# A token list of its own for the first expert tile in a mixture-of-experts encoder layer

## What is computed

```python
def hier_moe(h, w_group, w_router, w_exp_gate, w_exp_up, w_exp_down):
    gl = t @ w_group                       # 4 groups, top 1
    el = einsum('nd,gde->nge', t, w_router)  # 4 experts in a group, top 2
    ...
    for e in range(16):
        he = jax.nn.silu(t @ w_exp_gate[e]) * (t @ w_exp_up[e])
        out = out + dense_w[:, e:e + 1] * (he @ w_exp_down[e])
```

## Time and profile before

| | us |
|---|---|
| median of 3 runs (lowest to highest) | 902.66 (901.66 to 906.27) |
| the profiled execution | 903.54 |
| its span | 901.70 |
| TensorE busy (share of the span) | 867.5 (96%) |
| VectorE busy | 455.5 (51%) |
| ScalarE busy | 389.2 (43%) |
| GpSimd busy | 181.4 (20%) |
| moved by DMA | 142.47 MB, mean 158 GB/s |

### The profile page before, as it was taken

One profiled execution on the slowest core, in us unless ns is written; L12 is line 12 of the kernel. 1 busy time (PEld: TensorE's weight loads), 2 busy tenths in 40 slices (PEclk: granted clock), 3 DMA queues, 4 the chain that ended last, 5 costly groups with the idle time before them and its releaser, 6 DMA issues.

```text
span 901.7 us, 13646 instructions
## 1 busy us (share of the span) xinstructions
PE 867.5 (96%) x5206; PEld 731.5 (81%) x5206; DVE 455.5 (51%) x747; ACT 389.2 (43%) x539; POOL 181.4 (20%) x129
## 2 busy tenths in 40 slices
PE   8999999999999999999999999999988999899975
PEld 7988888898888888888888888888977878688842
DVE  5411356455519632324232147532588878787617
ACT  6432444444432543434334203124435677677613
POOL 0001010000100001100100001300013786778542
PEclk9999999999999999999999999999989999999998
DMA  9423132232220314321321112792859999988578
GB/s 295 124 69 77 48 76 65 60 69 56 59 71 18 94 47 77 85 63 47 64 61 34 60 47 95 242 395 94 303 195 329 361 381 381 385 306 293 199 258 338
DMA packets 97371, 142.47 MB, mean 158 GB/s; under 512 B 4582, under 2 KB 75446, under 8 KB 97238
## 3 DMA queue, kind: packets, MB, share of 16 engines
q1 hardware_dynamic: 89384, 115.05, 37.8%
q0 software_dynamic: 7904, 26.44, 10.5%
q10 hardware_dynamic: 32, 0.26, 0.3%
HBM read 116.31 MB, written 25.43 MB: 157 GB/s over the span
## 4 chain that ended last, share of the span: by engine, by line
PE 78%; DVE 6%; issue 4%; DMA 4%; SPq 3%; ACT 3%; POOL 2%; ACTq 0%; POOLq 0%; DVEq 0%
PE main L830 20%; PE main L831 19%; PE main L832 19%; PE work L914 3%; PE work L884 2%; PE work L947 2%; PE work L931 2%; PE work L901 1%; PE work L1061 1%; SPq L581 1%; PE work L1114 1%; DMA xg<-h_rows,column 1%; POOL e_lo0d L742 1%; DMA e_raw<-in_w_exp_down 1%; DMA x_in<-in_x_prompt 1%
## 5 line engine op out<-in xcount | busy, mean ns | idle before, releaser
L830 PE MATMUL main<-ht_hi,w_hi 128*128 128x512 f32 (+1 forms) x576 | 198.5, 345 | 0.0
L831 PE MATMUL main<-ht_lo,w_hi 128*128 128x512 f32 (+1 forms) x576 | 194.0, 337 | 0.0
L832 PE MATMUL main<-ht_hi,w_lo 128*128 128x512 f32 (+1 forms) x576 | 193.9, 337 | 0.0
L1512 DVE TENSOR_TENSOR w_lo<-raw,w_hi 128x2048 fp32r<-128x2048 f32 x29 | 66.4, 2290 | 234.9 <-ACT w_hi L1207 234.9
L830 PEld LDWEIGHTS main<-ht_hi,w_hi 128*128 128x128 f32 x576 | 109.2, 190 | 18.7 <-issue 5.2
L832 PEld LDWEIGHTS main<-ht_hi,w_lo 128*128 128x128 f32 x576 | 109.2, 190 | 11.9
L831 PEld LDWEIGHTS main<-ht_lo,w_hi 128*128 128x128 f32 x576 | 109.4, 190 | 10.9
L830 PE MATMUL main<-w_hi,ht_hi 128*128 128x256 f32 (+1 forms) x304 | 95.6, 315 | 0.1
L683 POOL DMA_DIRECT2D bias<-bias_vectors x16 | 12.4, 774 | 408.1 <-DVE nmx L1578 176.4
L832 PE MATMUL main<-w_hi,ht_lo 128*128 128x256 f32 (+1 forms) x304 | 92.9, 305 | 0.0
L831 PE MATMUL main<-w_lo,ht_hi 128*128 128x256 f32 (+1 forms) x304 | 92.8, 305 | 0.0
(11 more groups left out here) (276 smaller groups left out, 1557.1 us busy)
## 6 DMA issues: line engine op xcount, KB each, us to landing
e_raw<-in_w_exp_gate SPq DMA_DIRECT2D x16, 1024.0 KB, 8.6
e_raw<-in_w_exp_up SPq DMA_DIRECT2D x16, 1024.0 KB, 10.2
e_raw<-in_w_exp_down SPq DMA_DIRECT2D x16, 1024.0 KB, 8.7
raw<-in_w_in SPq DMA_DIRECT2D x30, 512.0 KB, 5.1
expert_rows<-y_sb SPq DMA_DIRECT2D x19, 512.0 KB, 8.6
raw<-in_w_in SPq DMA_DIRECT2D x8, 1024.0 KB, 5.1
expert_rows<-y_sb SPq DMA_DIRECT2D x1, 5632.0 KB, 22.7
raw<-in_w_out SPq DMA_DIRECT2D x4, 1024.0 KB, 5.8
```

Source lines behind the costliest of these rows:

```text
L830: pe.matmul(out, s_hi, m_hi, start=(first and i == 0), stop=False)
L831: pe.matmul(out, s_hi, m_lo, start=False, stop=False)
L832: last = pe.matmul(out, s_lo, m_hi, start=False, stop=(final and i == n - 1))
L1512: dve.tensor_tensor(w_lo[:, c % 2, :], raw[:, c % 2, :], w_hi[:, c % 2, :], ALU.subtract).then_inc(s_wlo, 1)
```

## The change

Six things are done:

1. The last tile's `rows2` moves from behind the one-hots to directly behind its `mean_inverse`, and so ahead of the logits.
2. VectorE takes the smaller of a token's two slot numbers (`lowest`) and compares it with 0..127 in one instruction (`hot_first`): a slot under 128 is a slot of tile 0. `tokens` holds the token numbers as fp32r, two equal columns. TensorE sums six products of it into `main[0]`, VectorE copies column 0 to `first_u`, and GpSimd gathers tile 0 by it after `s_firsttab`. The full table is made behind that, and tiles 1 and 2 are gathered by it.
3. TensorE's fill turns behind the first products are 8, and those behind the table products 24 instead of 48.
4. `turn_rows(0, 1)` goes into the middle of tile 0's gate and up product, behind 12 of its 24 matmuls.
5. ScalarE's `hidden_hi(0, 0)` goes ahead of the splits of tile 2.
6. VectorE does `rows_lo(0, 0)` ahead of the splits of tile 1's gate and up; the low half of tile 0's down weights goes from ahead of `tile(0, 0)` to behind `hidden(0, 0)`; then come `hidden_lo(0, 0)`, the splits of tile 2, and `route_weights` last.

```diff
+            dve.wait_ge(s_small, 16 * 9)
+            for i in range(2):
+                dve.tensor_copy(tokens[:, :, i], small[:, C_TOKEN:C_TOKEN + NT])
...
             mean_inverse(NT - 1)
+            rows2(NT - 1)
             dve.wait_ge(s_logit, NT)
-            dve.wait_ge(s_ss2, 2 * NT)
...
-            rows2(NT - 1)
...
             rt(dve.tensor_reduce(fl[:, :, :], both[:, :, :, :], AX.X, ALU.add))
+            rt(dve.tensor_tensor(lowest[:, :], fl[:, 0, :], fl[:, 1, :], ALU.min))
+            dve.tensor_tensor(hot_first[:, :, :], over(lowest[:, :], [P, NT, P], 2),
+                              over(small[:, C_IOTA:C_IOTA + P], [P, NT, P], 1), ALU.is_equal).then_inc(s_hotfirst, 1)
...
             rt(dve.tensor_copy(slots_f[:, :, :, :], slots_u[:, 1:3, :, :]))
+            dve.wait_ge(s_firstcol, 1)
+            dve.tensor_copy(first_u[:, :], main[0][:, 0:1]).then_inc(s_firsttab, 1)
```

On GpSimd and TensorE:

```diff
-            gp.wait_ge(s_tab, 1)
             for done in s_h2out:
                 gp.wait_ge(done, 16 * (NT // 2))
-            for j in range(3):
+            gp.wait_ge(s_firsttab, 1)
+            gather(0, 0)
+            gp.wait_ge(s_tab, 1)
+            for j in (1, 2):
                 gather(0, j)
             split_lo_part(0, 1, 2)
...
             spin(44)
+            pe.wait_ge(s_hotfirst, 1)
+            for t in range(NT):
+                last = pe.matmul(main[0][:, 0:2], hot_first[:, t, :], tokens[:, t, :], start=(t == 0), stop=(t == NT - 1))
+            last.then_inc(s_firstcol, 1)
+            spin(8)
...
             last.then_inc(s_table, 1)
-            spin(48)
+            spin(24)
...
+                if within:
+                    passes(gu_ps(par), pairs[:4], final=False)
+                    within()
+                    passes(gu_ps(par), pairs[4:], first=False).then_inc(s_gu, 1)
+                    return
...
             turn_rows(0, 0)
-            for j in range(3):
+            gate_up(0, 0, lambda: turn_rows(0, 1))
+            turn_hidden(0, 0)
+            for j in (1, 2):
                 tile(0, j)
```

On ScalarE and VectorE, in `tile` and ahead of it:

```diff
+                if not late(r, j, 1):
+                    hidden_hi(r, j)
                 split_expert(r, j + 2, (0, 1))
-                hidden_hi(r, j)
+                if late(r, j, 1):
+                    hidden_hi(r, j)
...
                 rows_lo(r, j + 1)
+                hidden(r, j)
                 if not late(r, j, 1):
+                    split_expert(0, 0, (2,))
+                    hidden_lo(0, 0)
+                    split_expert(0, 2, (0, 1))
                     route_weights()
-                hidden(r, j)
+                    return
...
+            rows_lo(0, 0)
             split_expert(0, 1, (0, 1))
-            rows_lo(0, 0)
-            split_expert(0, 0, (2,))
```

More of the change, by code:

```diff
@@ L330, in build @@
         gain3 = at("gain3", [P, D], F32, A_S + 8992)
-        assert A_S + 8992 + 4096 <= A_END
+        tokens = at("tokens", [P, NT, 2], F32R, A_S + 13120)
+        first_u = at("first_u", [P, 1], U32, A_S + 13184)
+        assert A_S + 13248 <= A_END
+        lowest = at("lowest", [P, NT], F32, A_S + 13216)
+        hot_first = at("hot_first", [P, NT, P], F32R, A_OA + 24576 + 4096)
         hot_slot = at("hot_slot", [P, 2, NT, P], F32R, A_BLK + 24576 + 12288)
@@ L407, in build @@
         s_hot_slot = sem("s_hot_slot")
+        s_hotfirst = sem("s_hotfirst")
+        s_firstcol = sem("s_firstcol")
+        s_firsttab = sem("s_firsttab")
         s_diffs = sem("s_diffs")
@@ L720, in gather @@
                 if isinstance(r, int):
-                    ids = table_u[:, j:j + 1]
+                    ids = table_u[:, j:j + 1] if j else first_u[:, :]
                 else:
@@ L1115, in turn_rows, with gate_up @@
                 last.then_inc(s_xtr, 1)
-            def gate_up(r, j):
+            def gate_up(r, j, within=None):
                 par = j % 2
@@ L1125, in gate_up @@
                 hi, lo = (w[par].rearrange("p c (k n) -> p k c n", k=KD) for w in (gate_up_hi, gate_up_lo))
-                passes(gu_ps(par), [((xt_hi[:, par, k, :], xt_lo[:, par, k, :]), (hi[:, k, :, :], lo[:, k, :, :]))
-                                    for k in range(KD)]).then_inc(s_gu, 1)
+                pairs = [((xt_hi[:, par, k, :], xt_lo[:, par, k, :]), (hi[:, k, :, :], lo[:, k, :, :]))
+                         for k in range(KD)]
+                if within:
[3 more added lines that the diff above has]
+                    return
+                passes(gu_ps(par), pairs).then_inc(s_gu, 1)
             def turn_hidden(r, j):
@@ L1902, in tile @@
                 rows_lo(r, j + 1)
+                hidden(r, j)
                 if not late(r, j, 1):
+                    split_expert(0, 0, (2,))
+                    hidden_lo(0, 0)
+                    split_expert(0, 2, (0, 1))
                     route_weights()
-                hidden(r, j)
+                    return
                 split_expert(r, j + 2, (0, 1))
-                if late(r, j, 1):
-                    copy_y(r, j - 1)
+                copy_y(r, j - 1)
                 hidden_lo(r, j)
+            rows_lo(0, 0)
             split_expert(0, 1, (0, 1))
-            rows_lo(0, 0)
-            split_expert(0, 0, (2,))
             for j in range(3):
```

## The result

The changed kernel took 910.14 us in the median of 16 runs (906.76 to 915.88), the kernel before 903.71 (900.34 to 906.47, also 16). The ratio is 1.0074 [1.0059, 1.0089]: slower by 6.7 us [5.3, 8.0]. The forecast was 903.8 with a range of 900.0 to 907.6; the time lies outside it, on the slow side. The profiled execution took 908.68 us, its span being 906.8.

What follows compares the result with a forecast made beforehand. The transfer queue was taken to set the end: gains of 0.7 and 4.05 us (T limited to 4.3) and 0.4 were absorbed by waits for transfers, and 1.1 us of later transfers gave 903.8 us, range 900.0 to 907.6.

Steps and rivals of the forecast that it cites:

- Step 1: Routing: last normalised rows moved to where their root is ready; slot numbers 0.7 us earlier.
- Step 2: First list behind the slot numbers: compare, six products and copy let the first gather start at 664.1, 4.05 us earlier.
- Step 3: Full table and fill turns: these turns set T, the start of the first tile's turns, at 669.9, 4.3 us earlier.
- rival B: Clock falls between 661.9 and 667.2, fill turns run at half clock: T 672.1 to 673.2, typically 906.6 us; chance 0.27.
- Step 4: Second tile's turns inside first gate/up: its end stays at T + 9.2; worth nothing, costs nothing.
- Step 5: VectorE's order behind gate/up: hidden values gain some 0.4 us, expert 0's down low half comes later, delaying three queues.
- chain of three queues: Behind expert 0's late down half: GpSimd's split T + 12.9 to T + 17.6, tile 3's gather 687.6, SP's down loads later.
- Step 6: Transfers from expert 3's down weights on: 3.5 us later, 2.3 made good by idle share, 1.1 us lost at the end.
- the late weights: Expert 3's down weights and later transfers 3.5 us late, 2.3 recoverable from idle share of 684 to 704 us.
- D: First gather isn't what T waits for, T held at 674.2; only the new order's lateness is left, 908.2 us; chance 0.04.
- C: Gain survives: tile 3's gather lands at 692.1, 2.7 us ahead, and the later stall shrinks: 899.9 us; chance 0.19.
- A: The forecast itself: clock stays up, transfers absorb the lead, 903.8 us; chance 0.50.

Runs made afterwards that it cites:

- e8: The changed kernel with its fill turns dealt out as 14, 5 and 12 for 8, 0 and 24; ratio 1.0026 to the kernel before.
- e6: e5 with fill turns dealt out as 14, 5 and 12 and the last rows back at their old place; ratio 0.9972 to the kernel before.
- e11: The kernel before with 64 fill turns for 44 ahead of the table products; ratio 0.999.
- e2: The kernel before with only VectorE's and ScalarE's new order (parts 5 and 6 of the change); ratio 1.0065, 5.9 us.
- e9: The kernel before with two unused GpSimd products laid over VectorE's splits of expert 2; ratio 1.0011.
- e12: The kernel before with 62 more fill turns, 6.9 us of TensorE's time, ahead of tile 3's turns; ratio 1.006, 5.4 us.
- e10: The kernel before with SP alone held back, so that only expert weights come late; ratio 1.003, 2.7 us.
- e4: The changed kernel with GpSimd's gathers first and its split waiting for VectorE's splits of expert 2; ratio 1.0099 to the kernel before.
- e7: e4 with the routing weights moved to the end of tile 2; ratio 1.0074 to the kernel before.
- e13: e6 once more, on another chip, beside the kernel before; ratio 0.9989.
- e5: The changed kernel with tile 0's down low half moved to behind the splits of expert 1; ratio 1.0017 to the kernel before.
- e1: The changed kernel with the edits to VectorE's and ScalarE's order (parts 5 and 6) taken back; ratio 1.0015 to the kernel before.

## Why the prediction was wrong

**Step 1 (rows moved up) failed.** The rows wait 1.26 us for the store of earlier rows, issued at 646.38, to give their buffer back, in front of the routing. The logits start at 654.10 where I had 652.8, and the slot numbers are ready 0.6 us later than before, where I had 0.7 earlier. I had read when the root is ready and not when the buffer is.

**Step 2 (first list) was right in kind.** The compare, the products (0.83 for my 0.8) and the copy cost what was said; with step 1's delay the gather starts at 665.59, 2.6 us earlier than before for my 4.05.

**Step 3 (T = 669.9) failed by rival B.** The clock fell right behind 667.8, after a stretch with TensorE busy 3.97 of 5.90 us and no gap over 0.9, and T at 674.02 lies beyond B's own 672.1 to 673.2. The arithmetic of step 3 was sound at full clock: e8 and e6 have 670.3 and 669.9.

The prediction quoted a rule there (the Trainium skill, TensorE: Matmul & The Clock Gate, Part 4: PE-mode transpose), by which the fill turns would hold no clock. The runs don't settle it. Against it stand the rise to 1.00 during fill turns alone, and e6 and e8, where the clock stayed at 1.00 with 31 of them between and behind 18 small products. But in the same two kernels the clock was 0.50 in fill turns from 652.90 to 655.60, with TensorE busy throughout 649.00 to 652.60, and in e11 it fell in the 48 turns.

**Step 4 held** nearly: the 24 matmuls end at 683.67, T + 9.6 for the 9.2 said.

**Step 5 is the step that failed, by a term left out.** The new order was priced at 1.1 us, and alone it costs 5.9 (e2). Its chain of three queues came out as worked: the down half at T + 10.9 (said 10.6), GpSimd's split from T + 13.3 to T + 17.9 (12.9 to 17.6), the gather of tile 3 at T + 18.0 (17.7). The gain of 0.4 us ahead of them didn't come: the hidden values are turned at T + 11.0 as before. And I timed GpSimd's split only against what waits for it by semaphore, and never laid it beside VectorE's row of the same microseconds. There stood the splits of expert 2, whose two inputs lie in SBUF. The hint was in the earlier trace rows: a 6-column operation of 3.04 us that "ends with GpSimd's split". I took it as an item removed from the path, a gain of 0.4, and not as the sign of a rule that the new order would meet with something larger. The Trainium skill (SBUF — State Buffer, Who interferes with whom) states it: a VectorE instruction with two SBUF inputs contends with a GpSimd instruction that reads SBUF, and the one that comes second is blocked for the whole of the first. The trace agrees, with 8.51 for 4.49 in after and the turns taken in e9. It was the rule against this change, and the prediction didn't weigh it. With the late gather beside it, it left TensorE 4.92 us idle, and the clock of 0.50 to 705.5 took 2.1 more.

**Step 6 was wrong as a model.** "The end is the end of this transfer queue plus a fixed rest" fell three times: in e12 5.4 of 6.9 us of TensorE's lag came through, in e8 and e6 some 4 of 4 us of lead. A share of 1.06 is what the loads look like when they are issued as early as freed buffers allow; the buffers are freed by the engines behind TensorE, so the queue is paced by them. e12's loads, issued 3 to 5.5 us later, show that they move with TensorE; that the freed buffer is the link is argued. The sign that the step named for its own failure, a share that isn't full, didn't show (1.05 in after). The step did foresee that tile 3 would wait for its gather: put 674.0 for its T, and its landing of 4.5 to 8.8 us gives 696.4 to 700.5, where 699.6 was measured. What it had wrong is that the queue takes such a lag away. Its one tested term, the late weights, costs 2.7 us by itself for 7.6 us of lateness (e10), where the step's rule (lateness less 2.3) gives 5.3.

**The rivals.** B named the clock, which explains why nothing was gained, and with it 906.6; but e2 has the loss with the old front, so B isn't its mechanism. D, given 0.04, had the nearest number, 908.2, from T at 674.2, which came true, and step 5 alone. Its number is near by luck: it priced late weights at 5.5, which e10 puts at 2.7, and it had neither hold nor half clock. C and A assumed T = 669.9. e8 is the change with that T, and its 1.0026 is 2.4 us where A said 1.1: near, but by two errors that cancel, a lead of 4 us that did reach the end and an order that costs 6. The losses don't add up (stall and half clock 7, late weights 2.7, together 6.7); that the late weights land while TensorE loses its time at tile 3 would explain it, but isn't shown.

**Left open**: what a hold of 4 us costs with no load late (e9 held 1.7, e4 and e7 were late as well), and how much of tile 3's lateness would stay with the hold gone and the gather as late as in after; what makes the clock fall (e6 and e13 are one kernel on either side of it, and e4, whose front is that of after, has T at 671.9 for 674.0); what e8 loses between tiles 12 and 13.

## What to carry to other kernels

When an instruction is moved, lay the new times of VectorE and GpSimd side by side, not only the semaphores: two such splits, one on each engine, ran one after the other here, and the group's mean is where it shows. When one late input is found, look when the others came; here the gathered rows landed 0.4 us before the turns began. A DMA share at its ceiling doesn't prove that transfers set the end; adding fill turns to the engine in question, as in e12, tells. Before a lead is counted, look up what else the moved instruction waits for, its output buffer too.

## What the runs showed of the hardware

- Which of the two engines is held depends on who starts first, and it is for whole instructions: 4.2 us under a 128x2048 split of GpSimd (after), 1.7 under a 128x1024 product (e9), and a 6-column operation is held like a large one (4.38 in e4), though it has one input in SBUF and a constant. Work of VectorE with one input in PSUM isn't: in e5, under GpSimd's split, `rows_lo` took 1.21 us and GpSimd's split 4.57, each its normal time. Nor is every operation on SBUF: in before, a reduce and a reciprocal ran at 0.17 and 0.19 us under the split of 679.04 to 683.65, right ahead of the one that was held. VectorE's timeline:

```profile
680.21 0.17 DVE L1856 TENSOR_REDUCE r<-r 128x6 f32<-128x24 f32 x1
680.41 0.19 DVE L1857 RECIPROCAL r<-r 128x6 f32<-128x6 f32 x1
```

- A gather's issue on GpSimd, 0.94 us, is held too: 2.81 at 692.06 and 1.90 at 695.18 under VectorE's splits in after. The second ends 0.8 us behind the group's end (697.08 for 696.26).
- The clock fell behind small products and fill turns (TensorE 3.97 us busy of 5.90, no gap over 0.9 us), in after, and once more in a single idle of 4.92 us, each time to 0.50. It also fell with no idle ahead: in e6, e8 and e1 TensorE was busy 3.60 of 3.60 us from 649.00 to 652.60, in products of 20 columns and transposes, and the clock is 0.50 from 652.90.
